# Hybrid decoder step on one core: expert loads in two halves, an earlier ranking, and wide products for the late attention groups

## The reference, cut to what matters

```python
# attention of the sample group: 8 sequences x 8 new tokens, 4096 cached keys each, top 256 kept
idx, valid = select_keys(indexer_scores(qi, wi, ki_all), q_pos, topk)
kg = where(is_past, cache_k[layer, phys, off], k_new[nidx])      # and vg likewise
logits = einsum('bqhd,bqkhd->bqhk', q, kg) * HEAD_DIM ** -0.5
p = softmax(where(valid, logits, -inf)); o = einsum('bqhk,bqkhd->bqhd', p, vg)
...
# mixture of experts: 576 tokens, 4 groups of 8 experts, the best 2 of the best group
combine = sum(one_hot(eid, 32) * gate)
hidden  = silu(einsum('nd,edf->nef', x, w_eg)) * einsum('nd,edf->nef', x, w_eu) * combine
ffn     = einsum('nef,efd->nd', hidden, w_ed)
ple     = sigmoid(x1 @ w_pg) * (p @ w_pp)
y       = layer_norm(ALPHA * x1 + ffn + ple)
```

## Time and profile before

| what | us |
|---|---|
| median of 3 runs (lowest, highest) | 1322.77 (1321.84, 1329.67) |
| the profiled execution, as timed | 1323.42 |
| its span in the trace | 1321.6 |
| PE busy, weight loads beside it | 1161.1, 729.8 |
| DVE, POOL, ACT busy | 744.8, 540.4, 432.7 |

### The profile page before, as it was taken

The page is one execution under the profiler, slowest core; times in us unless marked ns, Lnnn a source line. Parts: engine busy times, 40 slices in busy tenths (PEclk is TensorE's granted clock), DMA queues, the critical chain, the costliest instruction groups (busy, mean ns, idle before and its releaser), DMA issues.

```text
span 1321.6 us, 22136 instructions
## 1 busy us (share of the span) xinstructions
PE 1161.1 (88%) x8697; PEld 729.8 (55%) x8697; DVE 744.8 (56%) x1368; ACT 432.7 (33%) x952; POOL 540.4 (41%) x488
## 2 busy tenths in 40 slices
PE   5899999989896875779999999999979898969886
PEld 4435777777653433335566458888735454535442
DVE  1559999999989889797646133442611211111116
ACT  3541144455254467664131121231112222212120
POOL 5000087878777566666777000000113333323220
PEclk9899999989988877979999899999979899989888
DMA  9502222223366566667998620242378997799915
GB/s 325 206 29 67 64 64 64 66 86 116 110 169 181 168 170 193 205 213 219 304 308 253 219 96 22 73 150 80 123 309 347 381 398 316 302 364 380 420 61 203
DMA packets 81590, 258.59 MB, mean 196 GB/s; under 512 B 12799, under 2 KB 45427, under 8 KB 76679
## 3 DMA queue, kind: packets, MB, share of 16 engines
q1 hardware_dynamic: 50208, 168.79, 34.3%
q0 software_dynamic: 28720, 84.98, 20.2%
q10 hardware_dynamic: 2559, 3.40, 0.8%
HBM read 356.78 MB, written 19.05 MB: 284 GB/s over the span
## 4 chain that ended last, share of the span: by engine, by line
PE 41%; DVE 28%; DMA 18%; POOL 6%; issue 4%; ACT 1%; SPq 1%; DVEq 0%; POOLq 0%; ACTq 0%
DMA arena<-in_w_ex 14%; POOL arena L1048 6%; DVE arena L1941 6%; DVE arena L1940 6%; DVE arena L1942 6%; PE ps L1501 5%; PE ps L1118 5%; PE ps L1124 5%; PE ps L1348 4%; PE ps L1340 3%; PE ps L1522 2%; DMA arena<-in_cache_kv,arena 2%; DMA arena<-in_w_in 2%; PE ps L1206 2%; PE ps L1511 2%
## 5 line engine op out<-in xcount | busy, mean ns | idle before, releaser
L1048 POOL DMA_INDIRECT arena<-in_cache_kv,arena x256 | 267.5, 1045 | 117.9 <-issue 73.4
L1118 PE MATMUL ps<-arena 128*128 128x288 f32 (+2 forms) x1120 | 294.9, 425 | 1.1 <-ACT arena L1666 1.1
L1118 PEld LDWEIGHTS ps<-arena 128*128 128x128 f32 (+1 forms) x1120 | 209.9, 189 | 83.5 <-issue 30.3
L1501 PE MATMUL ps<-arena 128*32 128x256 f32 x2144 | 156.6, 414 | 46.3 <-DMA arena<-in_w_ex 45.3
L1074 POOL DMA_INDIRECT scr_ypair<-arena x67 | 66.9, 999 | 216.7 <-ACT arena L1874 212.3
L2337 DVE TENSOR_TENSOR arena<-arena,ps 128x64 f32<-128x64 f32 x67 | 14.8, 221 | 222.8 <-ACT arena L1868 222.8
L1501 PEld LDWEIGHTS ps<-arena 128*32 128x32 f32 x2144 | 65.8, 116 | 95.4 <-issue 60.1
L1589 ACT ACTIVATE arena<-ps 128x256 f32<-128x256 f32 (+5 forms) x138 | 57.7, 429 | 185.6 <-PE ps L1340 58.9
L1027 POOL TENSOR_TENSOR arena<-arena 128x816 f32<-128x816 f32 x58 | 103.0, 1775 | 18.1 <-ACT arena L1607 11.5
L1124 PE MATMUL ps<-arena 128*128 128x256 f32 (+4 forms) x544 | 107.6, 362 | 0.8 <-ACT arena L1811 0.6
L1068 POOL DMA_INDIRECT arena<-scr_x,arena x34 | 35.8, 1052 | 163.8 <-DVE arena L2316 153.3
(11 more groups left out here) (342 smaller groups left out, 1656.6 us busy)
## 6 DMA issues: line engine op xcount, KB each, us to landing
arena<-in_w_ex SPq DMA_DIRECT2D x68, 3072.0 KB, 11.5
arena<-in_w_in SPq DMA_DIRECT2D x20, 1024.0 KB, 5.7
arena<-scr_q SPq DMA_DIRECT2D x32, 256.0 KB, 4.4
arena<-in_cache_kv,arena POOLq DMA_INDIRECT x256, 3.8
arena<-in_w_o SPq DMA_DIRECT2D x4, 1024.0 KB, 6.9
arena<-in_w_pg SPq DMA_DIRECT2D x4, 1024.0 KB, 5.9
arena<-scr_ypair SPq DMA_DIRECT2D x4, 1024.0 KB, 7.9
arena<-in_x_prompt SPq DMA_DIRECT2D x4, 512.0 KB, 6.2
```

Of the source, the lines that this page charges most:

```text
L1048: pl.indirect_dma_start(unit_rows[:, 2 * j + t, half * H * HD:(half + 1) * H * HD], None, I["cache_kv"].rearrange("n (h d) -> (n h) d", h= ...
L1118: mm = nc.tensor.matmul(out, w[:, k], hT[:, k, a:b], start=(k == 0), stop=(k == KC - 1))
L1501: mm = nc.tensor.matmul(PS[2 + q % 2][r:r + BLK, 0:F], xT[:, p % 3, j, 64 * h + BLK * sub:64 * h + BLK * sub + BLK], w[:, 4 * h + j, half, ...
```

## The change

The loads of an expert become two DMAs with a semaphore each: the gate and up weights wait only for the up products of the visit six before, the down weights for its down products as before. The first three experts are loaded as soon as the table is there, ahead of the last `pp` weights. `rank`, DVE's table and the lists move ahead of the gates of groups 2 and 3. For the late attention groups, mask and new-key logits of 32 tokens at a time are made once by a job `lb` and kept in SBUF (`base_row`); a group then needs three products that pick its rows with `own_cols` and two wide ones for `kq`, whose sums stand in 32 columns a token.

```diff
@@ -368,6 +368,10 @@
 ATTENTION, VJOBS = merged([STREAM[k] for k in PICKS])[1:]
+LATE_TILES = (NGR - BY_VECTOR) * GQ * H // P
+_at = ATTENTION.index(("PT", BY_VECTOR - 1)) + 1
+ATTENTION[_at:_at] = [("lb", i) for i in range(LATE_TILES)]
+VJOBS.insert(VJOBS.index(("max", BY_VECTOR - 1)) + 1, ("tile_queries",))
 WO_ORDER = (0, 3, 1, 2)
@@ -410,7 +414,7 @@
     for pair in range(2):
-        jobs += [("pg", 2, t) for t in range(PT)] + [("rank",)] if pair else []
+        jobs += [("rank",)] + [("pg", 2, t) for t in range(PT)] if pair else []
         jobs += [("pg", 2 * pair + 1, t) for t in range(PT)] + [("pgS", pair)]
@@ -624,7 +628,13 @@
         prods = view(work_at + GQ * H * HD, (2, 2, H * HD))
-        kq = view(work_at + GQ * H * HD + 4 * H * HD, (2, 2, GQ, H))
+        kq = view(work_at + GQ * H * HD + 4 * H * HD, (2, 2, GQ, 32))
+        tile_at = work_at + GQ * H * HD + 2 * H * HD
+        tile_q = view(tile_at, (2, CC, P))
+        base_at = work_at + GQ * H * HD + 4 * H * HD + 4 * P
+        base_row = [view(base_at, (KEYS,)), kw.rearrange("p t c -> p (t c)")[:, 0:KEYS]]
+        assert base_at + KEYS <= work_at + GQ * CC * KEYS and LATE_TILES == 2
+        own_cols = C["w2mask"][:, 0:P]
         knew = view(b_end - CC * NS, (CC, NS))
@@ -810,7 +822,8 @@
         first_in = sem("first_in")
-        expert_in = [sem(f"expert_in{i}") for i in range(NSLOT)]
+        up_in = [sem(f"up_in{i}") for i in range(NSLOT)]
+        down_in = [sem(f"down_in{i}") for i in range(NSLOT)]
         xg_in = [sem(f"xg_in{i}") for i in range(XR)]
@@ -885,6 +898,23 @@
+            experts = I["w_ex"].rearrange("(e p) c -> e p c", e=NE)
+            UP = 2 * KC * F
+            asked = {}
+            def load_up(q):
+                if q >= NSLOT:
+                    sp.wait_ge(u_full, q - NSLOT + 1)
+                asked[q] = sp.value_load(widx[0:1, q:q + 1], min_val=0, max_val=2 * NE)
+                sp.dma_start(eset[q % NSLOT][:, 0:UP], experts[bass.ds(asked[q] % NE, 1), :, 0:UP],
+                             cond=(asked[q] < NE)).then_inc(up_in[q % NSLOT], 16)
+            def load_down(q):
+                if q >= NSLOT:
+                    sp.wait_ge(y_full, q - NSLOT + 1)
+                sp.dma_start(eset[q % NSLOT][:, UP:], experts[bass.ds(asked[q] % NE, 1), :, UP:],
+                             cond=(asked[q] < NE)).then_inc(down_in[q % NSLOT], 16)
             for n in range(WSLOTS, len(WGROUPS)):
@@ -919,26 +949,29 @@
                     sp.dma_start(eset[0], I["w_ex"][0:P, :]).then_inc(first_in, 16)
-                if not PG0 <= n < PG0 + WSLOTS:
-                    load_w(n)
-
-            def load_expert(q):
-                if q == 0:
+                if n == len(WGROUPS) - 1:
                     sp.wait_ge(table_ready, 1)
...
                     sp.wait_ge(first_in, 16)
-                if q == 3:
-                    sp.wait_ge(full, after("pp", 3, NT - 1))
-                if q == NSLOT - 1:
-                    sp.wait_ge(taken, TAKEN_AT[("pp", 3, NT - 1)])
-                if q >= NSLOT:
-                    sp.wait_ge(y_full, q - NSLOT + 1)
-                asked = sp.value_load(widx[0:1, q:q + 1], min_val=0, max_val=2 * NE)
-                sp.dma_start(eset[q % NSLOT], I["w_ex"].rearrange("(e p) c -> e p c", e=NE)[bass.ds(asked % NE, 1), :, :],
-                             cond=(asked < NE)).then_inc(expert_in[q % NSLOT], 16)
-
-            for q in range(NVISIT):
-                load_expert(q)
+                    for q in range(3):
+                        load_up(q)
+                        load_down(q)
+                if not PG0 <= n < PG0 + WSLOTS:
+                    load_w(n)
+            load_up(3)
+            sp.wait_ge(full, after("pp", 2, NT - 1))
+            load_down(3)
+            sp.wait_ge(full, after("pp", 3, NT - 1))
+            load_up(4)
+            load_down(4)
+            sp.wait_ge(taken, TAKEN_AT[("pp", 3, NT - 1)])
+            load_up(NSLOT - 1)
+            load_down(NSLOT - 1)
+            for q in range(NSLOT, NVISIT):
+                load_up(q)
+                if q > NSLOT:
+                    load_down(q - 1)
+            load_down(NVISIT - 1)
@@ -1165,23 +1198,27 @@
                     pe.wait_ge(bias_ready, 1)
+                if g >= BY_VECTOR:
+                    if g == BY_VECTOR:
+                        pe.wait_ge(drained, after("lb", LATE_TILES - 1))
+                        pe.wait_ge(own_cols_ready, 2)
+                    i, r = divmod((g - BY_VECTOR) * GQ * H, P)
+                    parts = (slice(0, P), slice(P, TOPS), slice(TOPS, KEYS))
+                    for t in (2, 0, 1):
+                        nc.tensor.matmul(PS[6][:, parts[t]], own_cols[r:r + GQ * H, :], base_row[i][r:r + GQ * H, parts[t]],
+                                         start=True, stop=(t == 2))
+                        if t == 0:
+                            pe.wait_ge(kq_done, (g - BY_VECTOR + 1) * GQ)
+                        if t < 2:
+                            mm = nc.tensor.matmul(PS[6][:, parts[t]], kq[:, g % 2, t].rearrange("p j r -> p (j r)"), ident,
+                                                  start=False, stop=True)
+                    mm.then_inc(lg_full, 1)
+                    return
                 for j in range(GQ):
...
                 pe.wait_ge(qz_ready, 2 * g + 2)
-                if g >= BY_VECTOR:
-                    for c in range(CC):
-                        for j in range(GQ):
-                            nc.tensor.matmul(PS[6][32 * j:32 * j + H, TOPS:KEYS], qz[:, g % 2, j, c, :], knew[:, c, :],
-                                             start=False, stop=False)
-                    pe.wait_ge(kq_done, (g - BY_VECTOR + 1) * GQ)
-                    for t in range(2):
-                        for j in range(GQ):
-                            mm = nc.tensor.matmul(PS[6][32 * j:32 * j + H, t * P:(t + 1) * P], kq[:, g % 2, t, j, :], ident,
-                                                  start=False, stop=(t == 1))
-                    mm.then_inc(lg_full, 1)
-                    return
                 pe.wait_ge(k_act, TURN[("T", g, GQ - 1, 1)] + 1)
@@ -1227,7 +1264,7 @@
                 kind, a = job[0], job[1:]
-                if job == ("pp", 2, 0):
+                if job == ("pg", 3, 0):
                     slot_lists()
@@ -1277,6 +1314,13 @@
                                           kiP[o:o + 64, 0:(t + 1) * P], start=True, stop=True)
+                elif kind == "lb":
+                    pe.wait_ge(tile_q_ready, 1)
+                    first = (BY_VECTOR * GQ * H + a[0] * P)
+                    nc.tensor.matmul(ps[:, 0:TOPS], C["qrow"][:, first:first + P], bias[:, 0:TOPS], start=True, stop=True)
+                    nc.tensor.matmul(ps[:, TOPS:KEYS], C["qrow"][:, first:first + P], bias[:, TOPS:], start=True, stop=False)
+                    for c in range(CC):
+                        mm = nc.tensor.matmul(ps[:, TOPS:KEYS], tile_q[:, a[0], c, :], knew[:, c, :], start=False, stop=(c == CC - 1))
                 elif kind == "oT":
@@ -1492,7 +1536,7 @@
                         pe.wait_ge(pre_ready, q - 1)
-                    pe.wait_ge(expert_in[q % NSLOT], 16 * (q // NSLOT + 1))
+                    pe.wait_ge(up_in[q % NSLOT], 16 * (q // NSLOT + 1))
                 w = up_weights(eset[q % NSLOT])
@@ -1514,6 +1558,7 @@
                 w = down_weights(eset[q % NSLOT])
+                pe.wait_ge(down_in[q % NSLOT], 16 * (q // NSLOT + 1))
                 pe.wait_ge(ht_ready, q + 1)
@@ -1752,6 +1797,10 @@
                     ins = hand_over(job, (a[0] // H + 1) * P, scale=ASC)
+                elif kind == "lb":
+                    if a[0]:
+                        act.wait_ge(st_out, 32 * NT)
+                    ins = nc.scalar.activation(base_row[a[0]], ps[:, 0:KEYS], cp)
                 elif kind == "oT":
@@ -2003,10 +2052,29 @@
+            V.memset(own_cols, 0.0).then_inc(own_cols_ready, 1)
+            dve.wait_ge(own_cols_ready, 1)
+            for r in range(0, P, GQ * H):
+                ins = V.tensor_copy(own_cols.rearrange("p (j r) -> p j r", j=GQ)[r:r + GQ * H, :, 0:H],
+                                    ident[r:r + GQ * H, r:r + GQ * H].rearrange("p (j h) -> p j h", j=GQ))
+            ins.then_inc(own_cols_ready, 1)
+            def tile_queries():
+                dve.wait_ge(lg_full, BY_VECTOR)
+                step(V.memset(view(tile_at, (2 * CC * P + 4 * P,)), 0.0))
+                for i in range(LATE_TILES):
+                    first = BY_VECTOR * GQ + i * (P // H)
+                    for e in range(2):
+                        o = 64 * e
+                        ins = V.tensor_copy(view(tile_at + i * CC * P + e, (CC, P + 2))[o:o + 64, :, 0:P:H],
+                                            qs[o:o + 64, :, first:first + P // H])
+                ins.then_inc(tile_q_ready, 1)
             def key_products(g, j):
                 k = (g - BY_VECTOR) * GQ + j
-                if k == 0:
```

(18 more changed lines are left out.)

## The result

| | before | after |
|---|---|---|
| median of the runs, us | 1322.69 | 1274.83 (1269.55 to 1279.3, 4 runs) |
| ratio after / before, 95% interval | | 0.9625 (0.9576 to 0.9675) |
| profiled execution, its span | 1323.42, 1321.6 | 1269.55, 1267.8 |
| first up products | 960.97 | 955.02 |
| last down products | 1281.16 | 1227.08 |

The kernel is 3.75% faster, 47.9 us by the medians; forecast were 1274 and a range of 1255 to 1298. The profiled execution is the fastest of its four. The two profiled ones differ by 53.9 us: 48.1 in the visits, 6.0 ahead of them, and -0.3 behind.

A forecast was written before the change was run, and what follows sets the result against it. Bound by the expert visits: 71.7 us lost, 45.3 waiting for weights, some 26 at half speed. 1323.42 - 46.9 (loads, earlier start) - 1.9 (attention) = 1274.6, median 0.65 lower: 1274 us; range 1255 to 1298.

The forecast's parts named there:

- The loads: Expert visits: up weights released sooner, down weights needed later; gain 46.9 us, 2.6 of it from the earlier first visit.
- the dense burst: Visits 43 to 62, 13 loads: 110 us at 8.4 us a load against 90 of PE work.
- the term for gaps: Visits 43 to 62: 2.6 us added for gaps in the load queue between bursts.
- The price of halves: Expert visits: waits for down halves and 67 more DMAs priced at 0; if uncovered, 2.8 us per burst.
- the 3.5 named as the sign of trouble: Expert loads: prediction wrong if 1024 KB halves land in a row more than 3.5 us apart.
- The order: Ahead of the visits: moved ranking, table and lists start the first up products at 958.4, 2.6 us sooner.
- PE's sum up to there is unchanged: Ahead of the first up products: PE's total work stays the same, rank's 4.88 us moving without costing more.
- The attention part: Late attention groups: 1.07 us each instead of 1.54, 1.9 us gained in all; bounds -4.5 to +3.
- (a): Expert visits: queue is the bound, 9.2 us a load, gain 30 or less, about 1292 us; chance 0.19.
- (b): Expert visits: 7.8 us a load, last burst 7 us shorter, about 1260 us; chance 0.12.
- (c): Expert loads: halves not pipelined, 2.8 us serially per transfer, some 20 us slower, 1342 us; chance 0.04.
- (d): Expert visits: early start alone counts, halves only reorder, about 1302 us; chance 0.09, mixes near it included.

The follow-up runs named there:

- e11: Changed kernel without expert loads, or waits for them, after visits 0 to 5; ratio 0.9471 to the kernel before, visits 247.5 us.
- e7: As e4, but each expert load as six transfers of 512 KB; ratio 0.9709 to the kernel before, visits 278.4 us.
- e6: As e4, but the up half is asked for only after the down products of the visit six before; ratio 0.9770 to the kernel before.
- e8: As e4, but each load in three transfers of 1024 KB, each with its own release and wait; ratio 0.9651 to the kernel before.
- e9: Changed kernel with a late attention group's five products as three; ratio 0.9658 to the kernel before, group 14 takes 1.28 us.
- e2: Kernel before with only ranking, table, lists and first loads moved ahead, loads whole; ratio 0.9969 to the kernel before, visits 314.6 us.
- e1: Kernel before with only the expert loads split in halves, order and attention as before; ratio 0.9741 to the kernel before, visits 284.2 us.
- e4: Changed kernel without the attention part, so split loads and new order only; ratio 0.9664 to the kernel before, visits 273.6 us.
- e3: Kernel before with only the attention part, the stored tile and five products; ratio 0.9978 to the kernel before (0.9954 to 1.0002).
- e10: Changed kernel run once more, nothing altered; ratio 0.9652 to the kernel before, visits 271.2 us.
- e12: Changed kernel with e9's three products and loads in three transfers, up weights stored for 8 KB rows; ratio 0.9618 to the kernel before.

## Why the prediction was right, and where not

**What bounds the kernel.** Right. e11 takes the loads away and the visits fall to 247.5 us; the forecast's split of the 71.7 us lost (45.3 waiting, 26 slow) is 72.7 (45.3 and 27.4).

**The loads.** Right in mechanism. Of the predicted 275.9 us between first up and last down, 272.1 came, by stretch: up 37 ended some 145 us after the first up products (143.6 predicted; the waits at 22, 27 and 28 are 3.8 us, against "2.2, with a slow restart 4"); visit 62 starts 105.7 us later, not 110; from there 21.5, not 22.3. The term that was mis-sized is the dense burst, and its price of a load: 8.4 us from two landings after a cold start, 8.13 in a queue that never empties (1120 to 1200, e7 above). 12.33 x 0.27 makes 3.3 of the 4.3 us. The remaining 0.9 is the term for gaps: 105.7 less 12.33 x 8.13 and the 3.8 leaves 1.7 for it, where I had added 2.6; the DMA share from 1099 to 1144, 0.97, has room for 1.4. Waits left in visits 45 to 62 are 10.0 us ("under 25"). The chain after runs through the load of visit 62, asked for at 1177.34:

```profile
1177.34 28.11 DMA arena<-in_w_ex
```

**The price of halves.** Right at 0: no down product waits, and e7 puts a transfer at 0.08 us at most. The rule weighed against it (the Trainium skill, DMA: Bandwidth & Descriptors, Anatomy of one DMA, some 2.0 us fixed, there for transfers that GpSimd issues) fits as completion time beside other transfers, which is how the page explains it: a lone load landed after 11.5 us, and in the burst one passes every 8.13; taken in series, 4 more for each of 30 loads, it would by estimate have cost e7 240 us, and it cost 4.8. In the burst 1024 KB pass every 2.7 us, a third of 8.13, below the 3.5 named as the sign of trouble.

**The order.** Right for the jobs that moved, not for PE's time ahead of them. From the start of the last ("pgS", 1) to the first up products it took 19.44 us (941.53 to 960.97), now 15.08 (939.94 to 955.02); 1.80 of this is `slot_lists`, moved ahead of that mark, which leaves 2.56 (2.6 predicted). First load at 918.2 (919). But from the start of the first ("pgS", 0) it took 66.80 us before and 65.86 after, so only 0.9 us arrived. These are its start before and after, and the window of `rank` after:

```profile
894.17 3.67 PE L1131 MATMUL ps<-arena 128*64 128x256 f32 x32
...
889.16 3.67 PE L1164 MATMUL ps<-arena 128*64 128x256 f32 x32
...
902.00:908.30 6.30, 6.30 (x42) 5.99 (x41) 1.28 (x4) 0.38 (x1) 0.00 (x0) 0.77 0.20 63
```

"PE's sum up to there is unchanged" failed here: `rank` took 6.28 us and not the 4.88 carried over the earlier trace rows, at a granted clock of 0.77, though PE had not paused since 893 and ran there at 1.00. Before, the clock was 1.00 around `rank` and 0.89 behind it. In e6 `rank` takes 4.99 with the slower stretch behind it, as before, and 64.36 pass; in e8 and e9, at full clock, 62.7. So the order brings 2.4 us at a clock like that of before, and between 0.9 and 4.1 from execution to execution; why the clock falls there is open. What I didn't see either is how much the early loads lean on the halves: alone it gives 5.6 us of visits (e2), on top of them 10.6 (e1 to e4).

**The attention part.** Here a step failed: "Now 5 products, 576 columns: 1.07 us." It was priced by columns, and each of the eight groups took 1.79. Before, four small products ran side by side, and my count had that right (832 columns, 1.54 us); but five full-width products are not bound by columns alone. So the groups became 0.25 us longer each, not 0.47 shorter. The two `lb` jobs ran from 551.03 to 554.2 with a wait of 1.53 ahead, and the later wait of 8.12 us is 4.41 now, so they were covered, as forecast. Against the bounds, -4.5 to +3, e3's interval says -6.1 to +0.3: it excludes the upper ones and doesn't decide the rest.

**The sum.** 1274.6 was made against the profiled execution and 1269.55 came: 3.8 us from the visits, 1.5 from the first up products (955.02, predicted 958.4 less 1.9), 0.3 the other way behind them; the match of the medians, 1274.83 to 1274, is closer than the steps were. The start's 1.5 is within the scatter: in fourteen profiled executions the first up products lie between 949.65 and 963.22, in e10, the same kernel, at 957.71. Of the 6.0 us gained ahead of the visits, at least 4.5 is clock, seen in two groups of the same products. Before:

```profile
753.54 6.52 PE L1340 MATMUL ps<-arena 128*128 128x512 f32 x8
...
858.32 19.23 PE L1124 MATMUL ps<-arena 128*128 128x36 f32 x96
```

After, the eight products (at 753.01) take 3.70 us and the 96 (at 854.98) 17.55. Another 0.9 is the order. The forecast had 4.5 us there from the steps themselves, 2.6 from the order and 1.9 from the attention part, so this part of the match, and with it the closeness of the medians (1274.83 to 1274), is luck. Why the clock differs between executions is open.

**The rivals.** (a), 9.2 us a load, is out: 8.13. (b), 7.8 us a load and 1260, was nearer in the price of a load than (a) but isn't reached. (c) is out by e7. (d), the early start alone, is out by e1 and e2.

## What to carry to other kernels

Where weights stream through slots, split a load by the instructions that read it, release each piece behind its last reader and await it ahead of its first: both sides gave some 11 to 30 us here, the less the fewer waits were left. Look up the price of a transfer in a burst where the queue never empties, not after a cold start, and when the DMA share reaches 1.00 stop splitting: thirds gave no time clear of the noise, and smaller rows lengthen a load. Count small PE products not by columns alone: the same 576 columns took 1.79 us in five products and 1.28 in three, and changes of the weights' height are the likely cause. Compare stretches from more than one mark: here the clock gave and took more than some of the steps.

## What the hardware showed that I had not expected

- In thirds the kernel loses less beyond its waits. e8 waits 20.1 us in pieces of at most 1.93 and loses 6.8 beyond, e12 14.5 in pieces of at most 2.73 and loses 7.8; e4 waits 13.5 in pieces of up to 3.99 and loses 12.6. From 1120 to 1200 the granted clock was 1.00 in e8, 0.98 in e12 and 0.94 in e4. These are single executions. The length of the one wait doesn't decide it: the 16 products right behind a wait took 1.93 us (1.2 GHz) after 2.54 us in e4, and 1.07 (full clock) after 3.86 before.
- The clock also falls while PE has no pause: 0.77 during `rank` in after, 1.00 in e8 and e9 in the same place.
- A change between weights of 32 rows and of 128 goes with some 0.25 us more, and the new weights are then loaded with their product and not ahead (group 14, above; argued, not isolated).
- Six transfers a load instead of two, with 4 KB a packet: 404 GB/s in the burst (e7, 1120 to 1200) against 419 (e4).
